# A two-layer streaming-encoder trunk on one core: two landing homes for weight chunks in place of three

## The reference, cut to what matters

```python
h = rms_norm(x, attn_norm[l])
z = h @ w_in[l]                      # 2048 x 3920 columns, split between two head groups
a_out = rms_norm(mla_mixer(...), mla_out_norm[l])   # latent attention: w_uq, w_ukv, 8 heads
g_out = gla_mixer(...)                              # gated linear attention, 4 heads
x = x + concatenate([a_out, g_out]) @ w_out[l]
h = rms_norm(x, ffn_norm[l])
u = causal_dwconv(h @ w_up[l], conv_w[l], conv_b[l])  # 2048 x 11264
x = x + (silu(gate) * up) @ w_down[l]                 # 5632 x 2048
```

## Time and profile before

| | |
|---|---|
| median of 3 runs | 2136.64 us (2135.44 to 2139.25) |
| profiled execution, its own time | 2138.89 us |
| its span, first to last instruction | 2137.0 us |
| mean granted TensorE clock | 0.999 |
| busy share: TensorE, VectorE, ScalarE | 100%, 72%, 47% |
| HBM read | 388.14 MB, 183 GB/s over the span |

### The profile page before, as it was taken

The page is one execution under the profiler, slowest core; times in us unless marked ns, Lnnn a source line. Parts: engine busy times, 40 slices in busy tenths (PEclk is TensorE's granted clock), DMA queues, the critical chain, the costliest instruction groups (busy, mean ns, idle before and its releaser), DMA issues.

```text
span 2137.0 us, 26593 instructions
## 1 busy us (share of the span) xinstructions
PE 2129.8 (100%) x11103; PEld 1825.0 (85%) x11103; DVE 1530.1 (72%) x1845; ACT 999.6 (47%) x1093; POOL 17.9 (1%) x22
## 2 busy tenths in 40 slices
PE   9999999999999999999999999999999999999999
PEld 8888788888888888888888887888888888888887
DVE  5666666877877778777756657678777877777776
ACT  6764545443443444443456645454344444344442
POOL 0010000000000000000001000000000000000000
PEclk9999999999999999999999999999999999999999
DMA  7654455555555555555554544555556555555553
GB/s 231 197 173 138 158 181 175 197 192 185 195 177 197 197 194 184 184 188 197 197 172 156 177 158 157 178 178 191 185 187 203 183 194 193 184 194 194 180 197 138
DMA packets 293853, 391.97 MB, mean 183 GB/s; under 512 B 11057, under 2 KB 200293, under 8 KB 293733
## 3 DMA queue, kind: packets, MB, share of 16 engines
q1 hardware_dynamic: 293172, 389.72, 55.3%
q10 hardware_dynamic: 176, 0.27, 0.1%
q0 software_dynamic: 384, 0.27, 0.1%
HBM read 388.14 MB, written 2.10 MB: 183 GB/s over the span
## 4 chain that ended last, share of the span: by engine, by line
PE 99%; ACT 0%; DMA 0%; DVE 0%; issue 0%; ACTq 0%
PE X L1445 15%; PE G L1445 15%; PE G L1358 12%; PE G L1360 12%; PE G L1359 12%; PE X L1452 8%; PE G L1452 8%; PE X L1360 4%; PE X L1359 4%; PE X L1358 4%; PE X L1427 1%; PE G L1396 1%; PE X L1670 0%; PE X L1727 0%; PE X L1738 0%; PE X L1696 0%
## 5 line engine op out<-in xcount | busy, mean ns | idle before, releaser
L861 DVE TENSOR_TENSOR lo<-raw,hi 128x2048 fp32r<-128x2048 f32 (+2 forms) x371 | 839.0, 2262 | 286.2 <-ACT hi L540 280.1
L540 ACT ACTIVATE hi<-raw 128x2048 fp32r<-128x2048 f32 (+2 forms) x371 | 702.1, 1893 | 615.1 <-PE G L1360 318.5
L1445 PE MATMUL G<-hx,hi 128*128 128x512 f32 x1408 | 336.2, 391 | 0.0
L1445 PE MATMUL X<-hx,hi 128*128 128x512 f32 x1408 | 335.8, 391 | 0.0
L1445 PEld LDWEIGHTS G<-hx,hi 128*128 128x128 f32 x1408 | 260.0, 188 | 51.1
L1445 PEld LDWEIGHTS X<-hx,hi 128*128 128x128 f32 x1408 | 258.8, 188 | 50.0
L1358 PE MATMUL G<-hi,hx 128*128 128x512 f32 (+1 forms) x480 | 187.8, 391 | 1.3 <-DVE lo L861 1.3
L1452 PEld LDWEIGHTS G<-hx,lo 128*128 128x128 f32 x1408 | 180.5, 191 | 6.9
L1452 PEld LDWEIGHTS X<-hx,lo 128*128 128x128 f32 x1408 | 180.5, 191 | 6.9
L1360 PE MATMUL G<-lo,hx 128*128 128x512 f32 (+1 forms) x480 | 183.4, 382 | 0.0
L1359 PE MATMUL G<-hi,hx 128*128 128x512 f32 (+1 forms) x480 | 183.0, 381 | 0.0
(11 more groups left out here) (267 smaller groups left out, 2248.7 us busy)
## 6 DMA issues: line engine op xcount, KB each, us to landing
raw<-in_w_up SPq DMA_DIRECT2D x176, 1024.0 KB, 5.1
raw<-in_w_down SPq DMA_DIRECT2D x88, 1024.0 KB, 5.0
raw<-in_w_in SPq DMA_DIRECT2D x55, 1024.0 KB, 5.2
raw<-in_w_out SPq DMA_DIRECT2D x32, 1024.0 KB, 5.0
raw<-in_w_uq SPq DMA_DIRECT2D x8, 768.0 KB, 4.6
raw<-in_w_in SPq DMA_DIRECT2D x8, 640.0 KB, 4.1
raw<-in_w_ukv SPq DMA_DIRECT2D x4, 1024.0 KB, 5.2
xk<-in_x SPq DMA_DIRECT2D x4, 512.0 KB, 8.0
```

Of the source, the lines that this page charges most:

```text
L540: act.activation(hi[:, k % SLOTS, 0:n], raw[:, k % SLOTS, 0:n], ACT.Copy).then_inc(hi_ready, 1)
L861: dve.tensor_tensor(lo[:, s, 0:n], raw[:, s, 0:n], hi[:, s, 0:n].bitcast(F32), ALU.subtract).then_inc(lo_ready, 1)
L1445: pe.matmul(bank2(un)[:, i, :], w_hi[:, at:at + P], hx[:, tile, :], start=tile == 0, stop=False)
```

## The change

`raw` gets a number of homes of its own, `LANDINGS` = 2, while `hi` and `lo` keep three. A load now waits for the lower part of chunk c - 2 in place of c - 3. ScalarE and VectorE read `raw` by k % 2 and write `hi` and `lo` by k % 3 as before. There is one landing semaphore for each of the two homes. Nothing else differs; line numbers are one higher behind the new constant.

```diff
+LANDINGS = 2
...
-        raw = sb("raw", [P, SLOTS, WORDS])
+        raw = sb("raw", [P, LANDINGS, WORDS])
...
-        raw_landed = [semaphore(f"raw_landed{s}") for s in range(SLOTS)]
+        raw_landed = [semaphore(f"raw_landed{s}") for s in range(LANDINGS)]
...
-                if c >= SLOTS:
-                    sp.wait_ge(lo_ready, c - SLOTS + 1)
-                return raw[:, k % SLOTS, :]
+                if c >= LANDINGS:
+                    sp.wait_ge(lo_ready, c - LANDINGS + 1)
+                return raw[:, k % LANDINGS, :]
...
-                act.wait_ge(raw_landed[k % SLOTS], (c // SLOTS + 1) * 16)
+                act.wait_ge(raw_landed[k % LANDINGS], (c // LANDINGS + 1) * 16)
                 if c >= SLOTS:
                     act.wait_ge(slot_free, c - SLOTS + 1)
-                act.activation(hi[:, k % SLOTS, 0:n], raw[:, k % SLOTS, 0:n], ACT.Copy).then_inc(hi_ready, 1)
+                act.activation(hi[:, k % SLOTS, 0:n], raw[:, k % LANDINGS, 0:n], ACT.Copy).then_inc(hi_ready, 1)
...
-                dve.tensor_tensor(lo[:, s, 0:n], raw[:, s, 0:n], hi[:, s, 0:n].bitcast(F32),
+                dve.tensor_tensor(lo[:, s, 0:n], raw[:, k % LANDINGS, 0:n], hi[:, s, 0:n].bitcast(F32),
                                   ALU.subtract).then_inc(lo_ready, 1)
```

More of the change, by code:

```diff
@@ L54 @@
 ACT_UNITS = (U_UKV + 1, U_UKV + 3, U_G, U_G + 1)
-assert DEPTH == 2 and CHUNKS % SLOTS == 0
+assert DEPTH == 2 and CHUNKS % SLOTS == 0 and CHUNKS % LANDINGS == 0
 G_ATTN, G_FFN, G_CQ, G_CKV, G_MLA, G_GLA, G_QN, G_KN = 0, 16, 32, 36, 38, 46, 48, 49
@@ L399, in load @@
                 dst = slot(l, k)[:, 0:n].rearrange("p (a b) -> p a b", a=shape[0])
-                sp.dma_start(dst, src).then_inc(raw_landed[k % SLOTS], 16)
+                sp.dma_start(dst, src).then_inc(raw_landed[k % LANDINGS], 16)
             def tokens(l, k, c0, which=range(4)):
@@ L437, in kv_chunk @@
                 sp.dma_start(dst[:, :, 0:KV_LORA + ROPE],
-                             w_in[l, :, 4 * q:4 * q + 4, C_CKV:C_CKV + KV_LORA + ROPE]).then_inc(raw_landed[(K_KV + q) % SLOTS], 16)
+                             w_in[l, :, 4 * q:4 * q + 4, C_CKV:C_CKV + KV_LORA + ROPE]).then_inc(raw_landed[(K_KV + q) % LANDINGS], 16)
                 sp.dma_start(dst[:, :, KV_LORA + ROPE:KV_WIDTH],
```

## The result

| | before | changed |
|---|---|---|
| median of 8 runs each | 2137.18 us (2135.44 to 2139.25) | 2143.85 us (2142.19 to 2145.66) |
| profiled execution, its own time | 2138.89 us | 2143.98 us |
| its span | 2137.0 us | 2142.2 us |
| mean granted clock | 0.999 | 0.999 |

The ratio of the changed kernel to the one before is 1.0029, 95% interval 1.002 to 1.0038: slower by 6.2 us, 4.3 to 8.1. The two medians are 6.7 us apart. The forecast was 2143.0 us.

A forecast was written before the change was run, and what follows sets the result against it. TensorE's own stream was taken as the bound, busy 2129.8 of 2137.0 us. Opening stalls of 4.7 us plus 1.7 us for the clock, 6.4 us put on the median, gave 2143.0 us; range 2136.5 to 2148.

The forecast's parts named there:

- No price in the steady stretches: All 264 MLP chunks and both layers' attention stretches: later loads were priced at 0.
- the tightest place: One MLP chunk whose load ScalarE would take 1.0 us late, with 5.3 us left before TensorE starts on it.
- Chunks 2 to 5 cost nothing: Opening: loads of chunks 2 to 5 go out later but cost 0; chunk 5 has 0.2 us to spare.
- The three stalls: Opening: TensorE waits 1.65 us before chunk 6, 1.0 before chunk 8, 2.1 before turning `c_tok`'s kv part; 4.7 us together.
- the bounds: Two load flights of 4.8 to 6.7 us vary the stalls by -0.6 to +3.2; with the clock, +4.1 to +9.6.
- The clock, +1.7 us: A half-clock stretch of about 3.4 us behind the third opening stall, priced at 1.7 us out of 0 to 1.7.
- A slow stretch ahead of a wait is eaten by the wait: Opening: a slow clock after the first or second stall costs nothing net, only eating into the next wait.
- the stalls come, the clock stays up: Rival: the opening stalls cost 4.7 us with no clock loss, 2141.3 us; chance 0.24.
- The one on two homes being as good as enough: Rival: opening loads fly in 4.8 us or less and the clock holds, +4.1 or less, 2140.7 to 2136.6; chance 0.20.
- The MLP rival: The 1.0 us lateness reaches TensorE once in each of 22 MLP groups, +22 us, about 2165; chance 0.08.
- the faster one: Rival: tiles moved in SBUF let TensorE read operands quicker on its 11103 matmuls, 2132 us or less; chance 0.03.
- The limit of 5.3 us in the MLP: MLP chunks: the cover from `hi` and `lo`'s third home is gone only if a load takes over 10.4 us.

The follow-up runs named there:

- the later series: The changed kernel run again unaltered, beside the kernel before on one chip: 2143.98 us against 2138.37, ratio 1.0028.
- the mirror: Two landing homes for chunks 0 to 11 and three from chunk 12 on, against the kernel before: 2143.69 us (2138.99), ratio 1.0025.
- the run that tried it: Changed kernel with each MLP load also waiting until TensorE is through with chunk c - 3: 2182.25 us, 38 us over the changed kernel.

## Why the prediction was right, point by point

- *No price in the steady stretches*: right, and to the size. The load at the tightest place was to be 1.0 us late and was 1.1; TensorE starts that chunk at the same distance as before. The run with three homes in the opening alone shows it from the other side.
- *Chunks 2 to 5 cost nothing*: right. The splits of chunks 2, 4 and 5 keep their times within the 0.1 us that TensorE is late before chunk 4. Chunk 5's load went out at 31.7, 0.6 us earlier than forecast.
- *The three stalls*: 1.65, 1.0 and 2.1 us were forecast, TensorE's idle gaps are 1.71, 1.00 and 1.79 us, and with the slower first matmuls behind them (0.47 us in place of 0.39 for the first of chunk 8) TensorE falls back by 1.8, 1.3 and 2.0 us. The kv part of `c_tok` was to be ready at 71.9 and was at 71.39 + 0.87 = 72.26. Sum: 4.7 forecast, 5.1 in the trace. The loads of chunks 8 and 10 each took 5.2 to 5.3 us from issue to landing (5.1 forecast). Chunk 6's load is a third one in the chain, and the bounds left it out; it landed at 43.3, 43.2 forecast. The queue behind the late instruction was the right thing to follow: moving one instruction took away two of the three stalls.
- *The clock, +1.7 us*: the term that was put wrongly. Neither profile of the changed kernel has a half-clock stretch behind the third stall, and the 5.1 us between the two profiled executions hold no clock term, since both have the stretch behind the old stall before chunk 4. That the size came out is luck. The profiled execution of before belongs to the slower of the two usual spans. I took its 2.25 us over the median for plain spread and put the price on the median; the median of before is 1.7 us under that execution (2137.18 against 2138.89), the median of the changed kernel lies on its own (2143.85 against 2143.98). So the 5.1 us of the trace became 6.7 us between the medians, and 5.6 in the later series, for another reason than the one priced.
- *A slow stretch ahead of a wait is eaten by the wait*: this holds in the changed kernel, as its two profiles show, and makes the kernel before the one that varies. The timelines give the likely reason: the chain starts at the lower part of chunk 4, ahead of the slow stretch. It is no rule for every wait. With the third home up to chunk 7 TensorE has two new waits behind the stretch too, but the chain that ends them starts when TensorE is through with chunk 4. There the runs at a clock of 1.0 and of 0.999 have medians of 2140.4 and 2142.6 us: the stretch is paid. With the absolute value moved, where the chain again starts at the landing of chunk 6, they have 2140.2 and 2140.5 us.
- *The sum*: 2143.0 forecast, 2143.85 measured, inside the range. Of the rivals, "the stalls come, the clock stays up" describes the profiled pair best, though its time, 2141.3, is 2.6 us off. The one on two homes being as good as enough fails as the kernel stands and holds once two steps are moved. The double buffering that the Trainium skill ("Trainium Kernel Development and Optimization", "Best Practices") asks for is enough in 360 of 372 chunks here, by the run above, and in the rest it depends on the order of the queues. The MLP rival and the faster one are out: no wait of TensorE in the MLP, TensorE's busy time is the same within 0.6 us, and the mirror, where nothing moves in SBUF, is as slow.
- *The limit of 5.3 us in the MLP*: as a statement on middle groups it stands; as one on all 264 MLP chunks it was wrong by 38 us in the run that tried it. The step that failed is that I measured the margin of a late load by the lower part alone, and not by what is queued behind it at the entry to the MLP and at its end.

## What to carry to other kernels

A buffer taken away costs nothing where a load's round trip fits the time between two uses, and the long steady loop is the easy part to check; look at the openings and the turns, where something that the bounding engine needs is queued behind a step that waits for the load. Price a late landing by the first such result, not by the wait it shows: here 150 us of new waits on ScalarE cost 5 us, and moving two steps past the waiting one made them almost free. Before a clock term is added, ask whether a later wait would eat it, which needs a chain that starts ahead of the slow stretch, and whether the kernel it is compared with has it in every run. A profiled execution that is 2 us off the median of its own runs is a reason to look at how those runs are spread, before a price is put on the median.

## What the runs showed of the hardware that I had not expected

The fall of the clock behind the same 1.3 us stall of the same program comes in some executions and not in others: from 39 to 42 us the two profiles of the changed kernel have a granted clock of 0.55 and of 1.00. On the same matmuls the stretch costs 1.5 us, a little less than the 1.7 us that I had worked out from the rows; the usual spans of the kernel before differ by 2.1 us, so the stretch is most of it, not all.

Nine of the profiles have the stall before chunk 4 (1.3 to 1.7 us). Five of them have the stretch, and in these chunk 4 starts between 38.68 and 38.87 us; in the four without, it starts between 38.06 and 38.62 us. What sets it was not tested. The three profiles without the stall have no stretch. In one of them, with chunk 4 moved alone, the same small transposes are in place, and none of its 11 runs had a mean clock under 0.999.
